# Values' third group: h split in the order of the tokens' remainders, and copied back for the queries

## The reference, cut to what matters

```python
h = rmsnorm(x, mix_pre_norm)
z = h @ w_in
qa, ka, va, ... = jnp.split(z, IN_OFFSETS, axis=-1)
# three groups of 8 heads, (window, dilation) = (128, 1), (512, 4), (2048, 16)
# a group with dilation d attends among the tokens of the same remainder: L, d = S // d, d
def to_sub(t):
    return t.reshape(B, L, dilation, Hg, hd).transpose(0, 2, 3, 1, 4)
```

## Time and profile before

| | |
|---|---|
| median of 3 runs | 1435.54 us (1435.31 to 1435.94) |
| profiled execution, its own time | 1436.18 us |
| its span, first to last instruction | 1434.4 us |
| TensorE busy in the span | 1426.7 us (99%) |
| VectorE busy | 937.3 us (65%) |
| ScalarE busy | 698.2 us (49%) |
| GpSimd busy | 24.1 us (2%) |
| values' second and third group | 378.0 to 425.15 us of the span |

### The profile page before, as it was taken

One profiled execution on the slowest core, in us unless ns is written; L12 is line 12 of the kernel. 1 busy time (PEld: TensorE's weight loads), 2 busy tenths in 40 slices (PEclk: granted clock), 3 DMA queues, 4 the chain that ended last, 5 costly groups with the idle time before them and its releaser, 6 DMA issues.

```text
span 1434.4 us, 21724 instructions
## 1 busy us (share of the span) xinstructions
PE 1426.7 (99%) x8356; PEld 1235.7 (86%) x8356; DVE 937.3 (65%) x1464; ACT 698.2 (49%) x1126; POOL 24.1 (2%) x43
## 2 busy tenths in 40 slices
PE   9999999999999999999999999999999999999998
PEld 7899999888898888888888888888889899888886
DVE  7988775435763555567867776764537888565975
ACT  5455555334533455555445554463345645434542
POOL 0000000000100000000000000000000000000000
PEclk9999999999999999999999999999999999999999
DMA  6333323334333222215422222223241432324653
GB/s 199 118 118 99 107 89 118 121 100 133 89 113 93 83 76 85 74 59 161 126 95 74 73 70 77 73 74 118 90 131 30 150 121 84 101 90 146 220 179 131
DMA packets 44325, 153.84 MB, mean 107 GB/s; under 512 B 5287, under 2 KB 5287, under 8 KB 44240
## 3 DMA queue, kind: packets, MB, share of 16 engines
q1 hardware_dynamic: 41472, 143.67, 31.2%
q0 software_dynamic: 2624, 8.95, 2.0%
q10 hardware_dynamic: 144, 0.04, 0.0%
HBM read 147.63 MB, written 4.23 MB: 106 GB/s over the span
## 4 chain that ended last, share of the span: by engine, by line
PE 97%; DVE 1%; DMA 1%; ACT 1%; issue 0%; SPq 0%; DVEq 0%
PE ps L517 20%; PE ps L519 19%; PE ps L518 19%; PE ps L684 4%; PE ps L685 4%; PE ps L686 4%; PE ps L2122 3%; PE ps L2123 3%; PE ps L2124 3%; PE ps L1175 2%; PE ps L1176 2%; PE ps L1177 2%; PE ps L2952 1%; PE ps L2522 1%; PE ps L2523 1%; PE ps L2524 1%
## 5 line engine op out<-in xcount | busy, mean ns | idle before, releaser
L463 DVE TENSOR_TENSOR wlo<-raw,whi 128x1024 fp32r<-128x1024 f32 x158 | 193.2, 1223 | 263.3 <-ACT whi L458 263.2
L517 PE MATMUL ps<-hh,whi 128*128 128x512 f32 x832 | 329.4, 396 | 0.0
L519 PE MATMUL ps<-hh,wlo 128*128 128x512 f32 x832 | 324.2, 390 | 0.0
L518 PE MATMUL ps<-hl,whi 128*128 128x512 f32 x832 | 324.1, 390 | 0.0
L458 ACT ACTIVATE whi<-raw 128x1024 fp32r<-128x1024 f32 x158 | 167.0, 1057 | 300.7 <-PE ps L519 274.9
L517 PEld LDWEIGHTS ps<-hh,whi 128*128 128x128 f32 x832 | 156.1, 188 | 36.9 <-issue 2.6
L519 PEld LDWEIGHTS ps<-hh,wlo 128*128 128x128 f32 x832 | 156.2, 188 | 33.2
L518 PEld LDWEIGHTS ps<-hl,whi 128*128 128x128 f32 x832 | 156.3, 188 | 31.0
L517 PE MATMUL ps<-ah,whi 128*128 128x512 f32 (+1 forms) x192 | 71.5, 372 | 0.0
L519 PE MATMUL ps<-ah,wlo 128*128 128x512 f32 (+1 forms) x192 | 71.3, 371 | 0.0
L518 PE MATMUL ps<-al,whi 128*128 128x512 f32 (+1 forms) x192 | 71.3, 371 | 0.0
(11 more groups left out here) (717 smaller groups left out, 3398.5 us busy)
## 6 DMA issues: line engine op xcount, KB each, us to landing
raw<-in_wstream SPq DMA_DIRECT2D x175, 512.0 KB, 3.5
w_raw<-in_wstream SPq DMA_DIRECT2D x46, 512.0 KB, 4.3
ring<-in_wstream SPq DMA_DIRECT2D x20, 512.0 KB, 4.3
xt<-in_x_t SPq DMA_DIRECT2D x16, 256.0 KB, 4.4
raw_early<-in_wstream SPq DMA_DIRECT2D x8, 512.0 KB, 4.4
raw_late<-in_wstream SPq DMA_DIRECT2D x4, 512.0 KB, 4.0
x_dram<-x_early POOLq DMA_DIRECT2D x4, 512.0 KB, 5.4
x_tok<-x_dram POOLq DMA_DIRECT2D x4, 512.0 KB, 5.7
```

Source lines behind the costliest of these rows:

```text
L463: nc.vector.tensor_tensor(wlo[:, s, :], raw[:, s, :], whi[:, s, :].bitcast(F32), ALU.subtract).then_inc(split_done, 1)
L517: nc.tensor.matmul(out, w, m, start=start, stop=False)
L518: nc.tensor.matmul(out, w, ml, start=False, stop=False)
L519: return nc.tensor.matmul(out, wl, m, start=False, stop=stop)
```

## The change

h, divided by its norm, is split into a second place, hp_high and hp_low, in which the tokens of a k-tile lie in the order of their remainders (4 x 128): VectorE's h_norm reads x and rstd with a step of four tokens and writes tmp without one, and the two halves are then made without steps. The third group takes its weights from there, side by side. For the queries and keys, ScalarE copies both halves of each k-tile back into hh and hl in the tokens' own order (`turned_back`): it reads without a step and writes with a step of four. These are 16 new instructions of 128 x 512. hp_low lies where the first group's weight blocks whi_v and wlo_v were. TensorE waits for all sixteen copies before the queries. Beside that, three semaphore counts of small tables are put into one, tables_in.

```diff
+        by_rest = "p (u r) -> p r u"
+        at[0] = arena + 51 * 1024
+        hp_high = [place(f"hp_high{i}", [P, R, U], F32R) for i in range(6)]
+        at[0] = arena + 68 * 1024
+        hp_high += [place(f"hp_high{i}", [P, R, U], F32R) for i in range(6, KT)]
+        at[0] = arena + 4 * S * (2 * FT + 1) + 4 * (2 * VEC + 3 * 32)
+        hp_low = [place(f"hp_low{i}", [P, R, U], F32R) for i in range(KT)]
...
-                        m = [x[:, kt, :].rearrange("p (u r) -> p r u", r=R)[:, t, :] for x in (hh, hl)]
+                        if g == 1:
+                            m = [x[:, kt, :].rearrange(by_rest, r=R)[:, t, :] for x in (hh, hl)]
+                        else:
+                            m = hp_high[kt][:, t, :], hp_low[kt][:, t, :]
...
-                        pe.wait_ge(sem("cst_in"), 16)
+                        pe.wait_ge(sem("tables_in"), 48)
...
-                nc.scalar.activation(hh[:, d, :], tmp[:, d % 2, :], ACT.Copy).then_inc(sem("h_high"), 1)
+                nc.scalar.activation(hp_high[d][:].rearrange("p r u -> p (r u)"), tmp[:, d % 2, :], ACT.Copy
+                                     ).then_inc(sem("h_high"), 1)
+
+            def turned_back(d):
+                act.wait_ge(sem("h_high"), IN_H + d + 1)
+                act.wait_ge(sem("h_low"), IN_H + d + 1)
+                for x, turned in ((hh, hp_high[d]), (hl, hp_low[d])):
+                    nc.scalar.activation(x[:, d, :].rearrange(by_rest, r=R), turned[:].bitcast(F32), ACT.Copy
+                                         ).then_inc(sem("h_turned"), 1)
...
                 if b > 1:
                     block_head(1, b)
+                    turned_back(2 * b - 4)
+                    turned_back(2 * b - 3)
                 h_head(2 * b)
                 h_head(2 * b + 1)
-            for b in range(3):
-                block_head(2, b)
+            block_head(2, 0)
+            for d in range(4, KT):
+                turned_back(d)
+            block_head(2, 1)
+            block_head(2, 2)
             leave(2, 0)
...
-                nc.vector.scalar_tensor_tensor(out=tmp[:, d % 2, :], in0=xt[:, d, :], scalar=PRE2[:, d:d + 1],
-                                               in1=rstd[:], op0=ALU.mult, op1=ALU.mult).then_inc(sem("h_norm"), 1)
+                nc.vector.scalar_tensor_tensor(out=tmp[:, d % 2, :].rearrange("p (r u) -> p r u", r=R),
+                                               in0=xt[:, d, :].rearrange(by_rest, r=R), scalar=PRE2[:, d:d + 1],
+                                               in1=rstd[:].rearrange(by_rest, r=R), op0=ALU.mult, op1=ALU.mult
+                                               ).then_inc(sem("h_norm"), 1)
...
             v_pe(pe)
             pe.wait_ge(sem("v_out0"), 2 * N_GROUPS + 1)
-            pe.wait_ge(sem("cst_in"), 16)
+            pe.wait_ge(sem("tables_in"), 48)
+            pe.wait_ge(sem("h_turned"), 2 * KT)
             attn_pe(pe)
...
-            act.wait_ge(sem("hot_in"), 32)
+            act.wait_ge(sem("tables_in"), 48)
```

More of the change, by code:

```diff
@@ L2602, in h_norm @@
                     dve.wait_ge(sem("h_low"), IN_H + d - 1)
-                nc.vector.scalar_tensor_tensor(out=tmp[:, d % 2, :], in0=xt[:, d, :], scalar=PRE2[:, d:d + 1],
-                                               in1=rstd[:], op0=ALU.mult, op1=ALU.mult).then_inc(sem("h_norm"), 1)
+                nc.vector.scalar_tensor_tensor(out=tmp[:, d % 2, :].rearrange("p (r u) -> p r u", r=R),
+                                               in0=xt[:, d, :].rearrange(by_rest, r=R), scalar=PRE2[:, d:d + 1],
+                                               in1=rstd[:].rearrange(by_rest, r=R), op0=ALU.mult, op1=ALU.mult
+                                               ).then_inc(sem("h_norm"), 1)
             def h_low(d):
                 dve.wait_ge(sem("h_high"), IN_H + d + 1)
-                nc.vector.tensor_tensor(hl[:, d, :], tmp[:, d % 2, :], hh[:, d, :].bitcast(F32),
-                                        ALU.subtract).then_inc(sem("h_low"), 1)
+                nc.vector.tensor_tensor(hp_low[d][:].rearrange("p r u -> p (r u)"), tmp[:, d % 2, :],
+                                        hp_high[d][:].rearrange("p r u -> p (r u)").bitcast(F32), ALU.subtract
+                                        ).then_inc(sem("h_low"), 1)
             for d in range(1, 4):
@@ L3723, in _ @@
             pool.wait_ge(sem(f"place_in{KT - 1}"), 16)
-            pool.dma_start(table[0:BUCKETS, :], rel_bias).then_inc(sem("hot_in"), 16)
-            pool.dma_start(hot_sb[:], onehot).then_inc(sem("hot_in"), 16)
-            pool.dma_start(cst[:], consts).then_inc(sem("cst_in"), 16)
+            pool.dma_start(table[0:BUCKETS, :], rel_bias).then_inc(sem("tables_in"), 16)
+            pool.dma_start(hot_sb[:], onehot).then_inc(sem("tables_in"), 16)
+            pool.dma_start(cst[:], consts).then_inc(sem("tables_in"), 16)
             pool.wait_ge(sem("vec_out"), 2)
```

## The result

The changed kernel takes 1439.28 us (median of 10 runs, 1437.47 to 1440.58) where the kernel before takes 1435.36 (10 runs on the same chip, 1434.59 to 1435.94): ratio 1.0027 [1.0018, 1.0035]. It is 3.9 us slower. Forecast were 1438.6 us, 1436.8 to 1441.6, and slower as the likeliest sign. The profiled execution took 1438.19 us, one of the shorter of the ten.

What follows compares the result with a forecast made beforehand. TensorE was taken to bound the kernel (97% of the chain that ended last). Waits of +3.1 and +0.35 less a gain of 0.45 summed to +3.0 us, on the median 1438.6 us; range 1436.8 to 1441.6.

Steps and rivals of the forecast that it cites:

- What bounds the kernel: TensorE bounds it; ScalarE's bank copies before the third group have no slack, so work ahead of them adds time.
- items 4 and 5: ScalarE's first four copies make TensorE's third group start 3.2 us later, 3.1 net; the next four cause no wait.
- item 4: ScalarE's first four copies, ahead of the h splits and bank copies: third group 3.2 us later, 3.1 net.
- Item 2: VectorE's eight norms, reading x and rstd with a step of four: 1.125 us each instead of 0.746.
- rival A: VectorE's stepped reads cost nothing: norms of 0.75 us, +1.5, 1437.1 us; chance 0.12.
- rival B: The two stepped reads of a VectorE norm hinder each other: norms of 2.0 us, +7.9, 1443.4 us; chance 0.12.
- Item 3: Sixteen ScalarE copies with stepped writes: the next starts 0.95 us later, between ends of 0.85 and 1.05.
- Rival C: Step free for copies and norms, so not slower: 1434.9 to 1435.4 us; needs copies of about 0.6 us; chance 0.06.
- Item 6: ScalarE's last eight copies delay the weight split feeding the third group's last quarter: TensorE waits 0.35 us.
- Item 1: Third group's weights side by side: 96 TensorE matmuls gain 0.15 to 0.65 us in all, -0.45 taken.
- Item 7: TensorE's wait for all sixteen copies before the queries, the joined semaphores and the queues cost nothing.
- rival D: TensorE's clock falls in the new 3 us wait: 2.9 us on top of +3.0, 1441.5 us; chance 0.10.

Runs made afterwards that it cites:

- plain_both: The changed kernel with VectorE's norms reading and ScalarE's copies writing without the step; 1434.84 us, ratio 0.9997 to the kernel before.
- in_gaps: The complete changed kernel, reordered: bank copies ahead of every stepped copy, copies back spread over ScalarE's gaps; 1434.81 us, ratio 0.9995 to the kernel before.
- after_again: The changed kernel run and profiled once more, no edit; 1439.14 us, ratio 1.0025 to the kernel before.
- after: The changed kernel itself, in its first runs and profile; 1439.28 us, ratio 1.0027 to the kernel before.
- plain_norms: The changed kernel with VectorE's norms reading x and rstd without the step, copies still stepped; 1436.50 us, ratio 1.0009 to the kernel before.
- wait3: The kernel before plus three idle plain copies on ScalarE ahead of the bank copies, nothing of the change; 1437.03 us, ratio 1.0011 to the kernel before.

## Why the prediction was right, and where it was not

**What bounds the kernel, and items 4 and 5: right.** The price came in at the wait that was named, behind ScalarE's v_tok. Counted with the 0.55 us by which this execution is early, the chain of item 4 is met step by step: the weight split at 398.49 (398.45 forecast), the first copy at 399.44 (399.4), the h split behind four copies at 403.18 (403.2), the bank copies through at 405.33 (405.45), the first matmul at 405.47 (405.7). The wait is 2.96 longer than before instead of 3.2. The missing 0.24 is the last piece, from the h split to TensorE: 2.3 us and not 2.5. The next four copies cost nothing, as said.

**Item 2: right.** A norm takes 1.14 us alone and 1.10 in a row; 1.125 was taken. Two stepped reads cost a norm as much as a stepped read beside a stepped write costs L3149. That ends rival A (0.75 us) and rival B (2.0).

**Item 3: right, at the lower edge.** 1.15 us for one copy, the next 0.92 to 0.94 later; 0.95 was taken, and of the two workings in the prediction the one by which stepped writes can't overlap gave 0.92. Rival C is ended by the same rows, and plain_both shows that its condition was put rightly: with copies of 0.61 us the kernel would not be slower.

**Item 6: wrong by its whole 0.35 us.** Eight copies took 419.11 - 411.77 = 7.34 us, where 7.6 was forecast, and the low half was ready 0.16 ahead of the matmul. The prediction had said that copies at 0.90 give no wait; between that and 0.95 lay the edge.

**Item 1: right.** Without a wait the stage is 0.43 (plain_both) and 0.45 (in_gaps) shorter, of which 0.08 is the first matmul that is no longer late; the gain in pace is 94 x (0.2348 - 0.2312) = 0.34. Forecast was 0.45, in bounds of 0.15 to 0.65. The 0.1 that item 4 takes off for the late matmul is not had in the changed kernel: behind the wait its first two matmuls are 0.31 apart (404.92 to 405.23), as before.

**Item 7: right.** The last copy ends at 419.4, 7.8 us ahead of the queries (7 forecast); no cost of the joined counts is seen.

**The sum, and rival D: the step that failed.** By the stage the change costs +2.6 us where the clock holds, and +3.0 was forecast: 0.35 too much in item 6 and 0.24 in the last piece of item 4, against 0.1 too little where the late matmul was taken off and 0.1 where the gain in pace was set too high. On top of it came the clock, 1.6 us in most executions (14 of 19 runs by their mean clock); this was rival D, with a chance of 0.10 and a price of 2.9. Its price was taken from the start of the span, half of 5.7 us at the lower level; behind the wait the level stays low for 3.0 us of matmuls. 2.6 + 1.6 = 4.2 is what the profiled execution of after_again shows, and the median, over executions with and without the loss, is +3.9. So the number 1438.6 came within 0.7 us of 1439.28 partly by luck, through two errors that pull against each other: 0.4 too much for the waits, and the clock left out. A forecast of the clock as part of the likeliest case would have been nearer for the right reason. The Trainium skill (TensorE: Matmul & The Clock Gate, Part 1: The HAM clock gate), which the prediction named, says that an idle engine is set back to 1.2 GHz; the trace of after_again agrees (matmuls 0.427 us apart behind the wait), the one of after, with the same wait, does not.

Small slips of rounding in its sums decide nothing: 396.91 + 1.5 is 398.41 and not 398.45, 403.2 + 2.23 is 405.43 and not 405.45, 1435.54 + 3.0 is 1438.54 and not 1438.6. It took 2.9 us as the least that can be told from no change; the interval of the ten runs is 1.2 us either way, so +3.9 is clear of it.

## What to carry to other kernels

A layout that spares TensorE a step can move the step to another engine, and that engine pays for it: here 0.36 us for each norm and 0.4 to 0.5 for each copy, against a few ns for each matmul. So before such an edit count what stands in the queue ahead of the next thing that TensorE waits for, and put the stepped work behind it; the same copies and norms cost 2.6 us of waiting and more in one place, and nothing that was seen in another. Where a new wait of TensorE is forecast that is as long as those behind which the clock fell here, the loss belongs into the sum itself, by the share of the runs that had it: 3 of 11 behind 2.1 us, 20 of 30 behind 2.8, all 5 behind 3.8. A single profile doesn't settle whether it comes, since two executions of one kernel, with the same wait, showed both.

## What the runs showed of the hardware

- A step of 16 bytes between float32 elements in SBUF cost some 0.4 to 0.5 us for 512 columns, on ScalarE, where it was written, and on VectorE, where it was read: they take 1.15 us instead of 0.61 as a ScalarE copy (0.92 instead of 0.52 from one start to the next), 1.14 instead of 0.75 as a VectorE operation that reads two operands with it. With two stepped reads a norm takes 0.39 us more, L3149 with a stepped read and a stepped write 0.38 more than plain work. TensorE's weight loads nearly hide it: 309 against 188 ns for a load, but 0.0036 us of pace.
- The granted clock fell to 1.2 GHz behind waits of 2.1, 2.8 and 3.8 us, not behind 1.3 us (two profiles, and none of 22 runs by the mean clock), and behind 2.1 and 2.8 us not in every execution. Each time the first two to five matmuls behind the wait ran at the higher level, then seven or eight at the lower. What the stage had lost beyond the wait itself, against a kernel without the wait, was 1.6 to 1.7 us, whether the wait had been 2.1 or 3.8 us; where the clock held (after, plain_norms, wait3) it was 0.1.
